# Down projection of a feed-forward layer by seven block products, with the remainders shared between VectorE and GpSimd

## What is computed

```python
D_MODEL = 2048
D_FF = 4 * D_MODEL
...
    h = h + o.astype(h.dtype) @ p['w_o']

    xm = rmsnorm(h, p['norm_mlp_g'])
    h = h + jnp.square(jax.nn.relu(xm @ p['w_up'])) @ p['w_down']
```

## Time and profile before

| | us |
|---|---|
| three runs | 3158.38, 3160.96, 3174.65 |
| median | 3160.96 |
| profiled execution | 3157.86 |
| span of its trace | 3156.1 |
| PE busy | 2948.2 |

### The profile page before, as it was taken

The page is one execution under the profiler, slowest core; times in us unless marked ns, Lnnn a source line. Parts: engine busy times, 40 slices in busy tenths (PEclk is TensorE's granted clock), DMA queues, the critical chain, the costliest instruction groups (busy, mean ns, idle before and its releaser), DMA issues.

```text
span 3156.1 us, 54227 instructions
## 1 busy us (share of the span) xinstructions
PE 2948.2 (93%) x22152; PEld 2754.0 (87%) x22152; DVE 1079.0 (34%) x1522; ACT 769.1 (24%) x931; POOL 1294.7 (41%) x593
## 2 busy tenths in 40 slices
PE   4889999857989999988999999999999999999997
PEld 4868788745679997766999999999999999999997
DVE  3668987857662233233222110011001110011213
ACT  2221111423443221111232221223112221122222
POOL 3256666344644432211434444443444444444441
PEclk9989999978999999999999999999999999999999
DMA  5422322573543355543333333333233333333332
GB/s 117 131 67 81 87 81 89 146 145 114 157 167 100 90 157 165 167 143 95 92 92 92 88 93 93 87 93 93 87 92 92 88 92 93 88 92 93 90 90 81
DMA packets 528784, 331.51 MB, mean 105 GB/s; under 512 B 56175, under 2 KB 479247, under 8 KB 527635
## 3 DMA queue, kind: packets, MB, share of 16 engines
q1 hardware_dynamic: 483856, 293.89, 32.1%
q10 hardware_dynamic: 44835, 36.31, 4.2%
HBM read 309.05 MB, written 21.40 MB: 105 GB/s over the span
## 4 chain that ended last, share of the span: by engine, by line
PE 74%; issue 9%; DVE 8%; POOL 5%; DMA 1%; ACTq 1%; SPq 1%; ACT 1%; POOLq 0%; DVEq 0%
PE lin L1182 67%; POOL wlo L666 4%; DVE rot L1622 3%; PE aux L1383 2%; PE aux L1361 1%; PE aux L1342 1%; ACTq L745 1%; PE aux L1333 1%; DMA s5p<-in_s_log_dt 1%; PE aux L1268 1%; SPq L557 1%; PE aux L1258 1%; DVE rot L1797 1%; DVE rot L1626 0%; DVE rot L1796 0%
## 5 line engine op out<-in xcount | busy, mean ns | idle before, releaser
L666 POOL TENSOR_TENSOR wlo<-raw,whi 128x1024 fp32r<-128x1024 f32 x472 | 1147.8, 2435 | 1673.7 <-ACT whi L742 1309.3
L742 ACT ACTIVATE whi<-raw 128x1024 fp32r<-128x1024 f32 x384 | 405.3, 1058 | 1547.1 <-PE lin L1182 1274.3
L1182 PE MATMUL lin<-mh,wlo 128*128 128x260 f32 x2048 | 412.8, 283 | 0.0
L1182 PE MATMUL lin<-fh,wlo 128*128 128x260 f32 x2048 | 412.8, 283 | 0.0
L1182 PE MATMUL lin<-mh,whi 128*128 128x260 f32 x2048 | 412.1, 282 | 0.0
L1182 PE MATMUL lin<-ml,whi 128*128 128x260 f32 x2048 | 412.1, 283 | 0.0
L1182 PE MATMUL lin<-fl,whi 128*128 128x260 f32 x2048 | 412.1, 283 | 0.0
L1182 PE MATMUL lin<-fh,whi 128*128 128x260 f32 x2048 | 411.9, 282 | 0.0
L1182 PEld LDWEIGHTS lin<-mh,whi 128*128 128x128 f32 x2048 | 315.9, 189 | 0.1
L1182 PEld LDWEIGHTS lin<-fh,whi 128*128 128x128 f32 x2048 | 315.8, 188 | 0.0
L1182 PEld LDWEIGHTS lin<-mh,wlo 128*128 128x128 f32 x2048 | 315.8, 188 | 0.0
(11 more groups left out here) (337 smaller groups left out, 4375.5 us busy)
## 6 DMA issues: line engine op xcount, KB each, us to landing
raw<-in_w_up SPq DMA_DIRECT2D x128, 512.0 KB, 4.0
raw<-in_w_down SPq DMA_DIRECT2D x128, 512.0 KB, 3.8
raw<-in_w_in SPq DMA_DIRECT2D x60, 512.0 KB, 3.7
raw<-in_w_v SPq DMA_DIRECT2D x32, 512.0 KB, 3.6
raw<-in_w_k SPq DMA_DIRECT2D x32, 512.0 KB, 3.5
raw<-in_w_out SPq DMA_DIRECT2D x32, 512.0 KB, 3.8
raw<-in_w_q SPq DMA_DIRECT2D x32, 512.0 KB, 5.8
piece<-in_cache_mem_k SPq DMA_DIRECT2D x32, 512.0 KB, 5.3
```

Source lines behind the costliest of these rows:

```text
L666: pool.tensor_tensor(wlo[:, slot, :], raw[:, slot % 2, :], whi[:, slot, :].bitcast(F32), ALU.subtract).then_inc(s.w_lo, 1)
L742: act.activation(whi[:, slot, :], raw[:, slot % 2, :], ACT.Copy).then_inc(s.w_hi, 1)
L1182: mm = pe.matmul(lin[:, 2 * i + f, 0:HALF], w, m[:, k, HALF * f:HALF * f + HALF], start=(n == 0 and part == 0), stop=(n == KT - 1 and part ...
```

## The change

**Shape.** The chunks are 1024 hidden features instead of 2048, so there are 8, each with N_UP = 4 up pairs and N_DN = 8 down pairs q. A down pair is now one 2 x 2 block product: the 1024 inner features in two halves, the 256 output features in two tiles m0 and m1, the tokens in two halves. With A the weight blocks and U the hidden blocks, seven products of 512 inner features, 128 outputs and 260 tokens take the place of eight. On the weights' side they need a11 twice in different states, a21, a12, a22, S1 = a21 + a22 and S2 = S1 - a11, and in place a21 = a11 - a21 and a11 = a12 - S2 (`sums`, on DVE, four instructions for the pair that comes next). On the hidden side DVE forms the seven blocks in uu while the up pairs run, ACT copies them to fh and DVE subtracts them into fl.

**Slots.** whi and wlo hold seven slots of 512 columns, one for each product 0 to 6 (`slot7`). ACT makes each whi slot from its source when PE has done the same product of the pair before (`hi_down`). POOL makes wlo of slots 0 to 4, DVE that of 5 and 6 (`lo_down` on each). A second pair of raw buffers, rawb, takes turns with raw. The up projection keeps its four units of 1024 columns.

**Banks.** Products 0, 2, 4 and 6 accumulate in one bank x, 1 and 3 in y, 5 in z; odd pairs use another set. Where a partial sum is needed by itself, ACT copies the bank out (`keep`, after products 0, 1, 2 and 4) and PE waits for the copy before it goes on with that bank: product 2 for the first copy, 3 for the second, 4 for the third, 6 for the fourth. DVE adds the four copies (`kept`) and the banks after products 3, 5 and 6 (`product`) to h.

**Elsewhere.** A few semaphores of the earlier parts are merged, and with them some waits come together (the three constant loads with the gains). The squares of the last chunk are made two tiles at a time and summed in ssf.

```diff
T_KV, T_OUT, T_Q, T_O, T_MLP = 15, 31, 39, 47, 55
-N_CHUNK = DFF // D
-T_END = T_MLP + 16 * N_CHUNK
+C_FF = 1024
+N_CHUNK = DFF // C_FF
+N_UP, N_DN = 4, 8
+U_MLP, U_C = 4 * T_MLP, 4 * N_UP + 7 * N_DN
+L_C = 4 * N_UP + 5 * N_DN
+F_C = 2 * N_UP + 3 * N_DN
...
-        fh = at("fh", [P, KT, TOK], R_B, F32R)
-        fl = at("fl", [P, KT, TOK], R_B + LO, F32R)
+        fh = at("fh", [P, 7, 4, HALF], R_B, F32R)
+        fl = at("fl", [P, 7, 4, HALF], R_B + 7 * 4 * HALF * 4, F32R)
+        uu = at("uu", [P, 8, HALF], R_B + 2 * 7 * 4 * HALF * 4)
+        sqf = at("sqf", [P, 2, TOK], R_A)
...
         rB = small("rB", [P, TOK])
+        W2 = here["at"]
+        rawb = at("rawb", [P, 2, 1024], W2)
+        s1 = at("s1", [P, 4, P], W2 + 8192)
+        s2 = at("s2", [P, 4, P], W2 + 10240)
+        ck = at("ck", [P, 3, HALF], W2 + 12288)
+        c_p1, c_p5, c_u2, c_u3 = ck[:, 0, :], ck[:, 1, :], ck[:, 2, :], uu[:, 7, :]
+        assert W2 + 12288 + 3 * HALF * 4 <= 229344
         ssq = small("ssq", [P, TOK])
         sqt = small("sqt", [P, TOK])
-        upr = at("upr", [P, TOK], here["at"])
...
+        def blocks(buf):
+            k1, k2 = (buf[:, k, :].rearrange("p (k n) -> p k n", k=4) for k in range(2))
+            return k1[:, :, 0:P], k2[:, :, 0:P], k1[:, :, P:2 * P], k2[:, :, P:2 * P]
+        def sources(buf):
+            a11, a12, a21, a22 = blocks(buf)
+            return a11, s1[:], s2[:], a11, a21, a12, a22
+        def slot7(t, i):
+            return t[:, i // 2, 512 * (i % 2):512 * (i % 2) + 512]
+        def quad(t):
+            return t.rearrange("p (k n) -> p k n", k=4)
+        raws = (raw, rawb)
+        def banks(par):
+            return ((lin[:, 0, 0:HALF], lin[:, 1, 0:HALF], lin[:, 2, 0:HALF]) if par == 0 else
+                    (lin[:, 3, 0:HALF], aux[:, 0, 0:HALF], aux[:, 1, 0:HALF]))
+        def hcol(m, f):
+            return flat(h)[:, bass.ds(TOK * m + HALF * f, HALF)]
+        def up_n(c, p, slot):
+            return U_C * c + 4 * p + (U_MLP + slot + 1)
+        def dn_n(c, q, i):
+            return U_C * c + 7 * q + (U_MLP + 4 * N_UP + i + 1)
...
-            with sp.Fori(0, N_CHUNK) as c:
-                with sp.Fori(0, 8) as p:
-                    load_pair(16 * c + p + T_MLP, io["w_up"], 2048 * c + 256 * p)
-                with sp.Fori(0, 8) as p:
-                    load_pair(16 * c + p + (T_MLP + 8), io["w_down"], 256 * p, 16 * c)
...
+            def load_down(c, q, par):
+                for k in range(2):
+                    if isinstance(q, int) and q == 0:
+                        sp.wait_ge(s.w_lo, L_C * c + (U_MLP + 4 * N_UP - 1 + k))
+                    elif k == 0:
+                        sp.wait_ge(s.w_lo, L_C * c + 5 * q + (U_MLP + 4 * N_UP - 5))
+                    else:
+                        sp.wait_ge(s.w_lod, 16 * c + 2 * q - 2)
+                    src = kp(io["w_down"])[:, bass.ds(8 * c + 4 * k, 4), bass.ds(256 * q, 256)]
+                    sp.dma_start(raws[par][:, k, :].rearrange("p (k n) -> p k n", n=256),
+                                 src).then_inc((raw_rdy, rawb_rdy)[par][k], 16)
...
+            def lo_down(c, q, par):
+                for i, src in enumerate(sources(raws[par])[0:5]):
+                    pool.wait_ge(s.w_hi, dn_n(c, q, i))
+                    pool.tensor_tensor(quad(slot7(wlo, i)), src, quad(slot7(whi, i)).bitcast(F32),
+                                       ALU.subtract).then_inc(s.w_lo, 1)
...
+            def hi_down(c, q, r, par, i):
+                if i in (0, 5, 6):
+                    k = 0 if i == 0 else 1
+                    if par == 0:
+                        act.wait_ge(raw_rdy[k], R_C * c + 16 * r + (32 * T_MLP + 32 * N_UP + 16))
+                    else:
+                        act.wait_ge(rawb_rdy[k], 64 * c + 16 * r + 16)
+                else:
+                    act.wait_ge(s.w_sum, 32 * c + 4 * q + (0, 1, 3, 4, 2)[i])
+                if isinstance(q, int) and q == 0:
+                    act.wait_ge(s.pe_unit, up_n(c, N_UP - 1, i // 2))
+                else:
+                    act.wait_ge(s.pe_unit, dn_n(c, q - 1, i))
+                act.activation(quad(slot7(whi, i)), sources(raws[par])[i], ACT.Copy).then_inc(s.w_hi, 1)
...
+            def down_period(c, q, par, after):
+                act.wait_ge(s.tile_free, F_C * c + 3 * q + (O_MLP + 2 * N_UP))
+                keep(c, q, 0, c_p1, par, 0)
+                after(0)
+                keep(c, q, 1, c_p5, par, 1)
+                after(1)
+                keep(c, q, 2, c_u2, par, 0)
+                after(2)
+                after(3)
+                keep(c, q, 4, c_u3, par, 0)
+                for i in (4, 5, 6):
+                    after(i)
...
+            def chunk(c, last):
+                with act.Fori(0, N_UP - 1) as p:
+                    for slot in range(4):
+                        hi_up(c, p + 1, slot)
+                    hidden_hi(c, p)
+                for i in range(7):
+                    hi_down(c, 0, 0, 0, i)
+                hidden_hi(c, N_UP - 1)
+                if not last:
+                    with act.Fori(0, N_DN // 2 - 1) as r:
+                        down_period(c, 2 * r, 0, then_down(c, 2 * r + 1, r, 1))
+                        down_period(c, 2 * r + 1, 1, then_down(c, 2 * r + 2, r + 1, 0))
+                    down_period(c, N_DN - 2, 0, then_down(c, N_DN - 1, N_DN // 2 - 1, 1))
+                    down_period(c, N_DN - 1, 1, lambda i: hi_up(c + 1, 0, {1: 0, 3: 1, 5: 2, 6: 3}[i]) if i in (1, 3, 5, 6) else None)
+                else:
+                    for q in range(N_DN):
+                        if q:
...
+            def down_pair(c, q, par):
+                x, y_, z = banks(par)
+                pe.wait_ge(s.tile_free, F_C * c + 3 * q + (O_MLP + 2 * N_UP - 1))
+                for i, (bank, opens, copied_) in enumerate(((x, True, 0), (y_, True, 0), (x, False, 1), (y_, False, 2),
+                                                            (x, False, 3), (z, True, 0), (x, False, 4))):
+                    if i < 5:
+                        pe.wait_ge(s.w_lo, L_C * c + 5 * q + (U_MLP + 4 * N_UP + i + 1))
+                    else:
+                        pe.wait_ge(s.w_lod, 16 * c + 2 * q + (i - 4))
+                    if copied_:
+                        pe.wait_ge(s.c_cp, 32 * c + 4 * q + copied_)
+                    if i == 5:
+                        pe.wait_ge(s.tile_free, F_C * c + 3 * q + (O_MLP + 2 * N_UP))
+                    for k in range(4):
+                        if par == 0 and k == 3:
+                            pe.wait_ge(s.hid_lo, 16 * c + (12 + (1, 1, 2, 3, 3, 4, 4)[i]))
+                        wh = slot7(whi, i)[:, P * k:P * k + P]
+                        wl = slot7(wlo, i)[:, P * k:P * k + P]
+                        for part, (w, m) in enumerate(((wh, fh), (wh, fl), (wl, fh))):
+                            mm = pe.matmul(bank, w, m[:, i, k, :], start=(opens and k == 0 and part == 0),
+                                           stop=(k == 3 and part == 2), skip_group_check=True)
+                    mm.then_inc(s.pe_unit, 1)
...
+                def hidden_lo(g, a, b):
+                    v.wait_ge(s.hid_hi, 16 * c + 4 * p + (g + 1))
+                    w = (slice(None), slice(a, b), bass.ds(p, 1), slice(None))
+                    step(v.tensor_tensor(fl[w].rearrange("p a b n -> p a (b n)"), uu[:, a:b, :],
+                                         fh[w].bitcast(F32).rearrange("p a b n -> p a (b n)"), ALU.subtract), s.hid_lo,
+                         (s.inv_done, 7) if g == 3 else None)
...
+            def sums(c, q, r, par, part):
+                a11, a12, a21, a22 = blocks(raws[par])
+                if part == 0:
+                    for k in range(2):
+                        if par == 0:
+                            v.wait_ge(raw_rdy[k], R_C * c + 16 * r + (32 * T_MLP + 32 * N_UP + 16))
+                        else:
+                            v.wait_ge(rawb_rdy[k], 64 * c + 16 * r + 16)
+                    lo_read(c, q, 1)
+                    tt(s1[:], a21, a22, ALU.add, s.w_sum)
+                    tt(a21, a11, a21, ALU.subtract, s.w_sum)
+                elif part == 1:
+                    lo_read(c, q, 2)
+                    tt(s2[:], s1[:], a11, ALU.subtract, s.w_sum)
+                else:
+                    v.wait_ge(s.w_lo, L_C * c + 5 * q + (U_MLP + 4 * N_UP + 1))
+                    tt(a11, a12, s2[:], ALU.subtract, s.w_sum)
...
+            def lo_down(c, q, par):
+                for i in (5, 6):
+                    v.wait_ge(s.w_hi, dn_n(c, q, i))
+                    tt(quad(slot7(wlo, i)), sources(raws[par])[i], quad(slot7(whi, i)).bitcast(F32), ALU.subtract, s.w_lod)
+            def kept(c, q, n, buf, m, f):
+                v.wait_ge(s.c_cp, 32 * c + 4 * q + n)
+                tt(hcol(m, f), hcol(m, f), buf, ALU.add)
+            def product(c, q, i, bank, m, f):
+                v.wait_ge(s.pe_unit, dn_n(c, q, i))
```

(18 more changed lines are left out.)

293 lines of the change are left out of this document (194 added, 99 removed).

## The result

| | before | changed |
|---|---|---|
| median, us | 3159.67 (4 runs, 3158.02 to 3174.65) | 3357.32 (4 runs, 3349.32 to 3362.67) |
| profiled execution, its span | 3157.86, 3156.1 | 3362.67, 3360.9 |
| ratio of the times | | 1.0612, interval 1.0573 to 1.0651 |

The changed kernel is 6.1% slower. The forecast was 3320, in a range of 3235 to 3390; the profiled execution is 44 us over the 3319 that the sum gave for it.

A forecast was written before the change was run, and what follows sets the result against it. PE was taken as the bound. Seven chunks 18.2 us longer each, the last 31, restarts 2 and tail 0.5 gave +161 us: 3157.9 became 3319, said as 3320, range 3235 to 3390.

The forecast's parts named there:

- The bound of before: Feed-forward layer: PE busy 200 of 200 us at full clock, helpers idle, 0.1202 us per 128x260 matmul.
- the cost of each part: Helpers' work per down pair: ACT 6.1 us, POOL 6.35, DVE 7.15, each under PE's 10.1.
- the signs that were named: Profile after: PE gaps, periods near 13.2 us, first near 20, DVE's two-SBUF instructions stretched, POOL's subtractions 1.27 to 1.8.
- The lock: SBUF port shared by DVE and POOL, one at a time; wanted 10.8 us a period against PE's 10.1.
- The order: Fixed queues in a down pair: PE idles from 8.8 to about 11.5 before product 6; period 13.2 us.
- DVE's gaps: Step between successive DVE instructions in a down pair, taken as 0.10 us.
- rival 3: The clock falls too with PE idle 3 of 13 us: +20 to +70, 3340 to 3390 us; chance 0.11.
- PE's restart: Delay when PE resumes after a wait in a down pair, taken as 0.15 us.
- POOL's first grant: In the down pair POOL asks for the port at 2.92 and gets it at 3.44 us.
- Rival 2: No lock that counts: helpers fit beside one another, PE runs 10.1 us a period, -76, 3085 us; chance 0.06.
- the laid-out period: One down pair timed engine by engine from PE's start on product 0: 13.18 us, where PE's own work is 10.1.
- Rival 1: Only the port's sum counts: a period costs 10.8 to 11.3 us, +55, 3215 us; chance 0.04.

The follow-up runs named there:

- Run 2: Changed kernel with POOL's five remainders of a down pair made for 32 of 512 columns only, the rest left out: 3199.14 us, ratio 1.0108.
- Run 3: Changed kernel with ACT's fourth copy moved ahead of slot 3's conversion, nothing left out: 3285.17 us, ratio 1.0393.
- run 6: Changed kernel with 16 idle matmuls into an unused bank ahead of PE's wait for the fourth copy: 3349.98 us, ratio 1.0597.
- run 5: Changed kernel, POOL's remainders cut to 32 of 512 columns, ACT's fourth copy before slot 3's conversion, last hidden blocks before slot 6: 3115.24 us, ratio 0.9852.
- run 7: Changed kernel with all seven remainders of a down pair on POOL instead of five: 3331.32 us, ratio 1.0534.
- run 9: Changed kernel, adds straight from PSUM, ACT's last hidden blocks earlier, DVE reordered with S1 before add 1, six remainders on POOL: 3193.11 us, ratio 1.0094.
- run 10: Changed kernel, adds straight from PSUM, ACT's last hidden blocks earlier, DVE reordered with S1 behind add 2, five remainders on POOL: 3160.56 us, ratio 0.9974.

## Why the prediction was right

The sign, the cause and the step at which PE stops were as forecast; the loss was 198 us where the sum had 161. Point by point:

- **The bound of before, and the cost of each part.** POOL's 128x512 took 1.28 (1.27 taken), ACT's 0.63 and 0.37 to 0.39 (0.63 and 0.42), DVE's 0.69 and 0.43, the transfers of w_down 3.5 to 3.7 us. All of these terms held, and so did the signs that were named: POOL's remainders are 1.26 at best and 1.71 at most, and the first period of a chunk is 19.7 to 21.0 (18.6 in the last), where 20.65 was laid out.
- **The lock.** The sums and adds with two SBUF operands show 0.69 and 0.43 at best, up to 1.45 on average in the groups that meet POOL and 1.82 at most, and the adds out of PSUM 0.43 throughout. Run 2 tests it by taking POOL's time away: 158 us, a part of which may be the clock's. DVE's sum ended 0.55 after POOL's instruction, whose own length is 0.69: about 0.14 of it lies outside the lock. By the Trainium skill (SBUF — State Buffer, "SBUF: two separate sides") whoever starts first has the pair of ports for the whole instruction; the trace agrees for POOL's, and for DVE's shows that much less than a whole one.
- **The order.** The wait before product 6, for the copy behind slot 3's conversion behind the fourth sum, was laid out as PE idle from 8.8 to 11.5, 2.7 us; it is 2.5 on average, 56 times. Run 3 takes it away and confirms it; it gave 72 us, for which I had expected half.
- **The mis-sized term: DVE's gaps.** The step "between DVE's instructions 0.10" holds for most, but not for all. The timeline shows 0.46 ahead of S1, 0.24 to 0.32 ahead of a kept copy, and 0.52 ahead of the remainders of every second pair (0.19 in the others). So a period at full clock is 13.5, not 13.18: 0.3 in six or seven periods, 2 us a chunk. That it is these gaps which make the 0.3 is added up, not tried by a run of its own.
- **The clock, rival 3.** I had it as a rival at 0.11. It came in part: in the chunk shown four of seven periods are under full clock and two of them are 14.5 and 15.0 us long instead of 13.5, some 2.9 us a chunk by run 6. Together with the gaps that is 4.9 of the 5.2 us by which a chunk (208.0 from one to the next) is over the forecast's 110.5 + 92.3 = 202.8. The first period is 1.0 shorter than laid out and the last with the up projection 1.0 longer, which cancel. Not every chunk is alike: from one to the next it is 205.5 to 208.3, the first, whose periods are all above 14 us by the ends of product 0, took some 4 us more, and the last is 213.9 where 215.9 was forecast. The layer is 33 us over its forecast of 1477.0 + 161 = 1638, and with the 9.2 us ahead of it, which are chance, that makes 43 of the 44 us. Against the medians the forecast is 37 us short, so some of the distance is that of a single execution.
- **Small slips.** The rows give 0.12 between DVE's instructions (0.10 was taken) and 0.19 for PE's restart (0.42 less 0.23; 0.15 was taken), and POOL's first grant, at 3.44, lies 0.07 ahead of the end of S1 at 3.51. None of them moves the forecast by much.
- **Rival 2 had a wrong price.** It said that without a lock the time is 3085. Run 2 has no lock worth the name and takes 3199, and only with ACT's order mended as well (run 5) is it under the kernel before, at 3115. I had priced it from the engines' sums, though the laid-out period shows that order alone holds PE up: the copy that PE needs stands behind DVE's fourth sum, and most of DVE's 13 instructions with their gaps stand in a row in front of that.
- **Rival 1** (3215) was not seen with the work whole: by the ends of product 0, no period of the changed kernel is under 13.28.

What made the change lose is settled to this extent: taking away POOL's long instructions gives 158 us, mending ACT's order 96, and both 242. How the clock's share of these, and of run 7's 26 us, splits off is not, and neither is why run 9 loses 33 us to run 10.

## What to carry to other kernels

This trade of matmuls for helpers' work was decided by the longest chain of hand-overs in a period, not by each engine's sum, so for the next one lay the queues out in order, with the waits that stand in front of what PE needs. If DVE and POOL both read SBUF tensors all the time, read accumulators straight from PSUM where DVE can, and put the instruction that frees a bank or an operand first in its queue and the preparation for the next period behind it. Here these two moves, with the last hidden blocks converted earlier, the norm's sums moved back and DVE's pairs written out, turned +6.1% into -0.7%.
